# First norm of a one-core decoder step: output weights and residual centred beforehand, variance per token spread by a diagonal product, router logits from the unscaled sum

## What is computed

```python
merged = g_a * y_a + g_b * y_b + g_c * y_c
m = einsum('bld,de->ble', merged, w_o)
h = layer_norm(ALPHA * x + m, ln1_g, ln1_b)      # mean and variance over the 1024 columns of a token
logits = h @ router_w + router_b                 # 16 experts, softmax, best group, top 2 of it
# 16 experts: silu(h @ w_gate[e]) * (h @ w_up[e]) @ w_down[e], then a second layer norm
```

## Time and profile before

| what | value |
|---|---|
| median of 3 runs | 1119.21 us (1118.0 to 1122.49) |
| the profiled execution, its own time | 1119.58 us |
| its span | 1117.8 us |
| PE, busy share of the span | 90% |
| DVE, ACT, POOL, busy share | 70%, 43%, 36% |
| DMA, mean over the span | 170 GB/s |
| last projection with `w_o` ends | 709.65 us |
| first product of the first expert starts | 763.63 us |

### The profile page before, as it was taken

The page is one execution under the profiler, slowest core; times in us unless marked ns, Lnnn a source line. Parts: engine busy times, 40 slices in busy tenths (PEclk is TensorE's granted clock), DMA queues, the critical chain, the costliest instruction groups (busy, mean ns, idle before and its releaser), DMA issues.

```text
span 1117.8 us, 19585 instructions
## 1 busy us (share of the span) xinstructions
PE 1004.2 (90%) x7141; PEld 903.3 (81%) x7141; DVE 781.9 (70%) x932; ACT 482.4 (43%) x666; POOL 402.1 (36%) x289
## 2 busy tenths in 40 slices
PE   6999999999998899999999979766999999999710
PEld 6999999999998889999999979634677777667500
DVE  2398888998898796634435443464989898878647
ACT  3222222222222342344422222454878788777511
POOL 2444444444544223444545435111221212122053
PEclk8999999999999899999999989977999999999865
DMA  7433332233332122333332366844999999995351
GB/s 200 112 95 94 94 91 87 86 93 94 95 94 76 38 82 68 121 94 94 94 92 80 92 212 221 305 156 147 331 368 392 372 390 368 387 383 211 119 208 61
DMA packets 169541, 189.88 MB, mean 170 GB/s; under 512 B 5875, under 2 KB 121587, under 8 KB 169484
## 3 DMA queue, kind: packets, MB, share of 16 engines
q1 hardware_dynamic: 162987, 177.46, 47.3%
q0 software_dynamic: 3008, 10.55, 3.0%
q10 hardware_dynamic: 3505, 1.36, 0.5%
HBM read 178.57 MB, written 11.76 MB: 170 GB/s over the span
## 4 chain that ended last, share of the span: by engine, by line
PE 76%; DVE 11%; DMA 5%; issue 3%; ACT 2%; SPq 1%; POOL 0%; POOLq 0%; DVEq 0%; ACTq 0%
PE pr L879 52%; PE pr L1017 13%; PE work L1017 7%; DMA y_rows<-y_out 3%; DVE acc_a L1201 2%; DMA sb_tok<-in_state_conv_b_dram 1%; PE work L1001 1%; DVE y_a L1492 1%; PE work L955 1%; DVE acc_b L1201 1%; PE work L964 1%; PE work L941 1%; DMA hs<-h_rows,ids 1%; SPq L385 1%; DVE w_up_lo L1400 1%
## 5 line engine op out<-in xcount | busy, mean ns | idle before, releaser
L519 POOL TENSOR_TENSOR w_lo<-raw,w_hi 128x512 fp32r<-128x512 f32 x224 | 303.4, 1375 | 394.5 <-ACT w_hi L620 394.5
L879 PE MATMUL pr<-x_hi,w_hi 128*128 128x260 f32 x1280 | 260.0, 284 | 3.1 <-POOL w_lo L519 3.1
L879 PE MATMUL pr<-x_hi,w_lo 128*128 128x260 f32 x1280 | 259.3, 284 | 0.0
L879 PE MATMUL pr<-x_lo,w_hi 128*128 128x260 f32 x1280 | 258.9, 284 | 0.0
L624 ACT ACTIVATE ev<-pr 128x520 f32<-128x520 f32 x104 | 63.0, 605 | 435.5 <-PE pr L879 435.5
L879 PEld LDWEIGHTS pr<-x_hi,w_hi 128*128 128x128 f32 x1280 | 199.4, 190 | 3.5 <-DVE x_lo L1116 3.3
L879 PEld LDWEIGHTS pr<-x_hi,w_lo 128*128 128x128 f32 x1280 | 198.8, 190 | 0.0
L879 PEld LDWEIGHTS pr<-x_lo,w_hi 128*128 128x128 f32 x1280 | 198.3, 190 | 0.0
L1168 DVE SCALAR_TENSOR_TENSOR work<-b_pad,par,work 128x512 f32<-128x512 f32 x224 | 148.2, 743 | 0.0
L620 ACT ACTIVATE w_hi<-raw 128x512 fp32r<-128x512 f32 x224 | 128.0, 623 | 5.3 <-DMA raw<-in_w_in_dram 2.8
L1400 DVE TENSOR_TENSOR w_up_lo<-w_up,ring 128x1024 fp32r<-128x1024 f32 x64 | 77.5, 1254 | 42.4 <-ACT ring L738 42.4
(11 more groups left out here) (237 smaller groups left out, 1689.7 us busy)
## 6 DMA issues: line engine op xcount, KB each, us to landing
raw<-in_w_in_dram SPq DMA_DIRECT2D x80, 512.0 KB, 3.7
w_gate<-in_expert_w_gate_dram SPq DMA_DIRECT2D x16, 2048.0 KB, 14.4
w_up<-in_expert_w_up_dram SPq DMA_DIRECT2D x16, 2048.0 KB, 13.9
w_down<-in_expert_w_down_dram SPq DMA_DIRECT2D x16, 2048.0 KB, 16.3
y_rows<-y_out SPq DMA_DIRECT2D x16, 384.0 KB
raw<-in_w_a_out_dram SPq DMA_DIRECT2D x8, 512.0 KB, 3.6
raw<-in_w_c_out_dram SPq DMA_DIRECT2D x8, 512.0 KB, 3.6
raw<-in_w_b_out_dram SPq DMA_DIRECT2D x8, 512.0 KB, 3.7
```

The costliest lines, as they stand in the source:

```text
L519: pool.tensor_tensor(w_lo[:, slot, k], raw[:, slot, k], w_hi[:, slot, k].bitcast(F32), ALU.subtract).then_inc(w_split, 1)
L879: mm = pe.matmul(pr[slot][:, h, 0:HALF], w[:, slot, k, :], x[:, k, h * HALF:(h + 1) * HALF], start=(k == 0 and w is w_hi and x is hi), sto ...
```

## The change

1. `w_o` is no longer loaded as 8 raw tiles. SP loads it whole, as two transfers of 2 MB (`wo[0]` in `CB`, `wo[1]` in `V`), after the first two raw loads of `N_GB` and after a wait for `b_split`; the other 14 raw loads of `N_GB` follow.
2. DVE centres the weights: in the merges 3 to 6 of `N_GB`, two of the 8 blocks each, it sums a row of 1024, scales the sum, and subtracts it from the row. ACT and POOL round and split `w_o` from there.
3. The residual is centred beforehand: its blocks are summed in the merges, PE takes the mean between the first two projections with `w_o`, DVE subtracts it. So the sum z = residual + projection has mean zero per token. DVE adds each projection from PSUM to it; ACT squares each block, DVE sums the squares.
4. The variance is taken per token (tokens on partitions, products of 2 columns), root and reciprocal on 128x5 numbers, and five diagonal matrices spread the result over all partitions by a product.
5. The router's logits are taken from z with weights times gain; scale per token and the router's shift (a product of its own) are added on DVE after the transposes.
6. ACT loads its table for the root earlier, rounds the first gate matrix after the copies of `h`, and takes the logits out after two of the eight gains. SP issues the expert loads in another order, and the stores of `h` before three of them.

```diff
@@ SP
-            pairs(N_GB, G_B, b_out_v)
+            load(0, N_GB, in_v, G_B)
+            load(1, N_GB + 1, b_out_v, 0)
+            sp.wait_ge(b_split, KB)
+            for h in range(2):
+                sp.dma_start(wo[h][:], o_v[:, h * KB // 2:(h + 1) * KB // 2, :]).then_inc(wo_in, 16)
+            with sp.Fori(1, KB) as o:
+                load(0, o * 2 + N_GB, in_v, o * P + G_B)
+                load(1, o * 2 + (N_GB + 1), b_out_v, o * P)
@@ ACT
+            def round_wo(i):
+                act.wait_ge(proj_done, N_WO + i + 1)
+                for h in range(2):
+                    k = slice(h * KB // 2, (h + 1) * KB // 2)
+                    act.wait_ge(wo_centred, KB // 2 * (h + 1))
+                    act.activation(w_hi[:, i % 2, k], wo[h][:, :, i * P:(i + 1) * P], ACT.Copy).then_inc(w_rounded, 1)
...
-            singles(N_WO, 32, 8, last=True)
+            act.activation(agg[0:1, 0, 0:1], eps_t[0:1, 0:1], ACT.Sqrt).then_inc(std_ready, 1)
+            for i in range(KB):
+                if i < KB - 1:
+                    round_wo(i + 1)
+                act.wait_ge(z_ready, i + 1)
+                act.activation(ev[i % 4][:], m[:, i, :], ACT.Square).then_inc(sq_ready, 1)
@@ PE
-            singles(N_WO, q_hi, q_lo)
-            pe.wait_ge(summed, 5)
-            mean("meanH", sums)
+            for i in range(KB):
+                if i >= 2:
+                    pe.wait_ge(z_ready, i - 1)
+                project(i % 2, N_WO + i, q_hi, q_lo, wait_free=i < 2)
+                if i == 0:
+                    pe.wait_ge(summed, 5)
+                    mean("meanX", sums)
...
+            logits((0, 1))
+            pe.wait_ge(summed, 6)
+            for b in range(NTB):
+                n = P if b < 4 else TS
+                mm = pe.matmul(pr[1][0:n, 0, 2 * b:2 * b + 2], sums[:, b * P:b * P + n], mean_w[:, 0:2], start=True, stop=True)
+            mm.then_inc(tok_var, 1)
+            logits((2, 3, 4))
+            pe.wait_ge(diag_ready, 1)
...
+                    mm = pe.matmul(pr[1][:, half, at_col:at_col + hi - lo], mean_w[0:n, :], diag[0:n, b, lo:hi], start=True, stop=True)
+            mm.then_inc(r_spread, 1)
+            mm = logits((5, 6, 7))
             for k in range(KB):
+                mm = pe.matmul(pr[0][:, 1, 272:272 + E], mean_w[:], rw_b[:, k, :], start=(k == 0), stop=(k == KB - 1))
@@ DVE
+            def centre_weights(k):
+                part, col_k = wo[k // 4][:, k % 4, :], w_mean[:, k:k + 1]
+                do(dve.tensor_reduce(col_k, part, AX.X, ALU.add))
+                settle()
+                do(dve.tensor_scalar(col_k, col_k, 1.0 / D, None, ALU.mult))
+                settle()
+                dve.tensor_scalar(part, part, col_k, None, ALU.subtract).then_inc(wo_centred, 1)
+            for o in range(KB):
+                merge(N_GB, o, o % 2, "last")
+                settle()
+                if 3 <= o < 7:
+                    dve.wait_ge(wo_in, 32)
+                    for k in (2 * o - 6, 2 * o - 5):
+                        centre_weights(k)
+            for i in range(KB):
+                dve.wait_ge(proj_done, N_WO + i + 3)
+                to(x_centred).wait()
+                mi = m[:, i, :].rearrange("p (h t) -> p h t", h=2)
+                do(dve.tensor_tensor(mi, mi, pr[i % 2][:, :, 0:HALF], ALU.add), to(z_ready))
```

More of the change, by code:

```diff
@@ L18 @@
-from contextlib import ExitStack
+from contextlib import ExitStack, nullcontext
 import concourse.bass as bass
@@ L757, in _ @@
                 act.activation(h_tok[b][:].rearrange("p (h t) -> p h t", h=2), work[TILE[f"ht{b}"]][0:n], ACT.Copy).then_inc(h_tok_ready, 1)
+            rounded_parts(first, "gate", 0, 0, 0, free=range(CH))
             def tokens_in(ps, m, t):
@@ L1296, in _ @@
                     t.leave(KB // 2)
-            looped = ((chain, 8), (gates, 2), (to(merged_split), 2))
-            with dve.Fori(0, KB // 2) as i:
-                for t, n in looped:
-                    t.enter(i, n)
-                for b in range(2):
-                    merge(N_GB, i * 2 + b, b, "last")
-                    settle()
-                for t, _ in looped:
-                    t.leave(KB // 2)
-            for i in range(KB):
-                dve.wait_ge(evacuated, N_WO + i + 3)
-                do(dve.tensor_tensor(m[:, i, :], m[:, i, :], ev[2 * (i % 2)][:], ALU.add), gates)
-                if i:
-                    settle()
-                    do(dve.tensor_tensor(sums[:], m[:, 0, :] if i == 1 else sums[:], m[:, i, :], ALU.add), chain if i < KB - 1 else to(summed))
@@ L1319, in _ @@
-            settle()
+                do(dve.tensor_tensor(mk, mk, work[TILE["meanX"]][:, :, 0:HALF], ALU.subtract), to(x_centred))
+            for i in range(KB):
+                dve.wait_ge(proj_done, N_WO + i + 3)
+                to(x_centred).wait()
+                mi = m[:, i, :].rearrange("p (h t) -> p h t", h=2)
+                do(dve.tensor_tensor(mi, mi, pr[i % 2][:, :, 0:HALF], ALU.add), to(z_ready))
+                if i >= 2:
+                    dve.wait_ge(sq_ready, i)
+                    settle()
+                    do(dve.tensor_tensor(sums[:], ev[0][:] if i == 2 else sums[:], ev[(i - 1) % 4][:], ALU.add))
@@ new lines, in _ @@
+            dve.wait_ge(sq_ready, KB)
+            settle()
+            do(dve.tensor_tensor(sums[:], sums[:], ev[(KB - 1) % 4][:], ALU.add), to(summed))
+            dve.wait_ge(tok_std, 2)
+            do(dve.reciprocal(r_tok[:, 0:4], r_tok[:, 0:4]))
+            do(dve.reciprocal(r_tok[0:TS, 4:5], r_tok[0:TS, 4:5]))
+            settle()
+            for b in range(NTB):
+                n = P if b < 4 else TS
+                ins = dve.tensor_scalar(diag[0:n, b, 0:n], ident[0:n, 0:n], r_tok[0:n, b:b + 1], float(D), ALU.mult, ALU.mult)
+                if b < NTB - 1:
+                    do(ins)
+                else:
+                    ins.then_inc(diag_ready, 1)
```

149 lines of the change are left out of this document (85 added, 64 removed), and 2 rows, old and new, of the table ROUNDS.

## The result

| | kernel before | changed kernel |
|---|---|---|
| median | 1119.28 us (1118.0 to 1122.49, 4 runs) | 1130.25 us (1125.8 to 1132.7, 4 runs) |
| ratio, 95% interval | | 1.0092 (1.007 to 1.0115) |
| the profiled execution, its span | 1119.58, 1117.8 us | 1125.8, 1124.0 us |
| eviction of `N_GB` | 567.56 | 564.29 |
| eviction of `N_GB`+2 | 580.01 | 590.50 |

What follows compares the result with a forecast made beforehand. PE bounds the kernel except from the last `w_o` projection to the first expert, where steps follow each other. Terms 14.2 + 0 + 3.5 - 11.4 = +6.3 us give 1125.5 in the median's terms; range 1116 to 1134.

Steps and rivals of the forecast that it cites:

- Term 1: Start of the `N_GB` pairs: third raw tile, queued behind the 4 MB of `w_o`, lands late and idles PE; +14.2 us.
- Rival A: At `N_GB`+2, DMA engines serve the raw tile beside the 4 MB, no hold-up; 1111.8 us, faster; chance 0.10.
- Term 2: Merges of the `N_GB` pairs: centring `w_o` on DVE costs 0 us, two effects in the last pair cancelling; ends -1, +5.5.
- rival B: Branch B's pairs: DVE becomes the bound through slow sums or subtractions waiting for POOL; +5.5, 1131 us; chance 0.13.
- estimate of 2.1 from the strided row: DVE's centring sum of 1024: 2.1 us as other end, at the rate of a sum read across blocks; 1.15 taken.
- Term 3: Projections with `w_o`: mean products 0.9 us, then PE idles 2.7 us once before the third projection; +3.5 us.
- Term 4: Last projection to first expert product: shorter end of the norm, 53.98 us becoming 42.6; -11.4 us, ends -8 and -15.
- The expert stage: Experts after the norm: 0 us, since their matrices land well before needed and PE remains the bound.
- the better ends of the four terms: Most favourable end given for each forecast term, from the `w_o` load to the first expert; said to give 1119 to 1121.
- rival C: Norm gives more than counted or the raw-tile stall is shorter; 1119 to 1121 us, no difference; chance 0.15.

## Why the prediction was right, and where its sum was off

**Term 1, +14.2: right, +13.8.** The tile landed at 580.7, 14.6 us after its issue; the forecast had 15.8. PE waited 11.8 us (11.3 put down, 11.5 by the prediction's own lines). The clock's share was there but smaller: PEclk was 0.50 up to 586 and 0.85 from 586 to 588, so PE worked some 3.9 us at the lower level, which costs 2.0 us and not 2.9. The added transfer alone gave the same 13.8 in the kernel before. Its picture of a tile served behind the transfer holds for one queue, as here. Rival A, that the engines serve the tile beside the 4 MB, does happen when the two are in different queues, and gains nothing: 350 packets of the tile go beside 352 of `w_o`, and a packet of the tile is an eighth of the other's bytes.

**Term 2, 0: mis-sized, +0.9.** The prices were right: the sum 1.22 us for 1024 (1.15 forecast), the subtraction 0.75 (0.8), and 1.48 where POOL worked beside it. So rival B fell, and with it the estimate of 2.1 from the strided row. What the term cancelled did not cancel: it expected the last merge to come clear of POOL, but the late centring put POOL's low part of the next tile right onto it. PE starts 0.9 us later behind the last projection than in the kernel before (6.5 us against 5.6), where the merge met POOL in part (sum 1.53, cast 1.28, `q_lo` 0.70 us in its timeline); without the centring it starts 2.3 us sooner than there.

**Term 3, +3.5: right in the sum, +4.0, but with luck in it.** The gap of 2.7 us, ended by POOL, is there to the tenth, and the mean products cost 1.0 (0.9 put down). Two effects of the clock, which the sum left out, almost cancel. The third projection, behind the gap, took 7.4 us and not 5.8 (PEclk 0.50 from 690 to 692 us): +1.6; closing the gap gave 3.7. And the first projection took 7.35 us where before took 8.7: -1.3. There PEclk was 0.50 up to 666 and 0.85 from 666 to 668, 6 us behind PE's start; here it was 0.66 from 674 to 676 already, so the lower level ended 3.4 us behind the start.

**Term 4, -11.4: the step that failed, -7.3.** The first part holds: gains at 17.4, table load at 18.7. From POOL's quarter to the first product it is 11.7 us (11.8 forecast), but by luck, as two errors cancel: the gather's instruction is 2.9 us shorter, its transfer beside the expert loads 3.8 us longer, where I had put down 1.0. Two sums were too small. The copies of `h` took 7.0 us after the load, not 5.75: PE had stood idle for 3.8 us ahead of the transposes, the clock from 742 to 748 us was 0.58 where before it was 1.00, and ACT waited 1.7 us for them, before 0.2. That is 1.3. No run here takes that idle time away, so this share is read from the trace and not tested. And POOL's quarter was put at 2.52, its time in a stretch where DVE was not in such work; in its new place it runs beside DVE's 3.49 us of low parts and takes 5.45. That is 2.9. Together 4.2, and the term was 4.1 short. The expert stage was 0 within the spread of the profiles.

One sum in the rivals is off: the better ends of the four terms (12, -1, 2.5, -15) give 1117.7, and rival C says 1119 to 1121. The forecast does not rest on it.

So three of four terms came out within 1 us each, two of them with errors inside that cancel, and the sign rested on term 1: the norm's shortening is real, 7.3 us, and it is outweighed by a transfer placed a few instructions too early.

## What to carry to other kernels

A large early load is paid for by whoever loads small packets at the same time, on any queue; put it behind the tiles that are due next, and in pieces. When a step moves, take its duration from a stretch with the same neighbours: here DVE and POOL slowed one another by a factor of two and more, and PE's work behind idle gaps of 2.7 and 3.8 us ran in part at the lower clock (0.62 and 0.58). Before a saved stretch is counted, look at what else was hiding in it.

## What the runs showed that I had not expected

- Two queues at once moved equal numbers of packets (352 and 350 in 4 us), so with 4 KB against 0.5 KB the small-packet tile got an eighth of the other's bytes.
- POOL's gather instruction depends on DVE: 1.12 us alone, 4.04 beside three two-input subtractions, in the kernel before too (4.04 at 753.00 in its timeline). A row with one duration for instruction and transfer hides which of the two it is.
- The gather's 96 rows of 4 KB took 3.04 us behind its instruction at 131 GB/s on the engines, and 6.86 at 371. My estimate from these two is that holding the expert loads back until it has landed might give some 3 us; no run here shows it.
- A cast on DVE with one input took 1.48 us beside POOL and 0.43 alone.
- The exponential began 0.02 us after the end of its table load (742.55 + 1.28 = 743.83, then 743.85), with no further wait.
- The start of the stage `N_GB` differs by up to 6 us between executions of kernels that are the same up to there. One profile against one profile would have given +6.2 for this change; the medians gave 10 to 11.
